# Weights of 512-column groups stored with two 128-column blocks interleaved, for a two-block transformer kernel on TensorE

## The reference

```python
mod_l = jax.nn.silu(c) @ w_ada + b_ada                    # 2048 x 12288, one row
p     = modulate(rms_norm(x, g), sh_a, sc_a) @ w_in       # 2048 x 3904
x     = x + gt_a * (merged_heads @ w_out)                 # 2048 x 2048
x     = x + gt_f * ((a * silu(g)) @ w_down)               # up 2048 x 11008, down 5504 x 2048
z     = rms_norm_2(x, norm_mix_g_2) @ w_in_2              # 2048 x 10248
x     = x + (sigmoid(g_a) * (att_a @ w_proj_a) + sigmoid(g_b) * (att_b @ w_proj_b)) @ w_out_2
x     = x + square(relu(hm @ w_up_2)) @ w_down_2          # 2048 x 8192 and back
```

## Time and profile before

| | |
|---|---|
| three timed runs | 2705.6, 2709.5, 2710.15 us |
| median | 2709.5 us |
| profiled execution, first to last instruction (its span) | 2701.8 us |
| busy: PE, weight loads, VectorE, ScalarE | 96%, 93%, 65%, 45% of the span |
| granted TensorE clock, mean | 0.984 |
| matmuls in the record | 21322 |
| HBM | 548.5 MB read, 204 GB/s over the span |

### The profile page before, as it was taken

One profiled execution on the slowest core, in us unless ns is written; L12 is line 12 of the kernel. 1 busy time (PEld: TensorE's weight loads), 2 busy tenths in 40 slices (PEclk: granted clock), 3 DMA queues, 4 the chain that ended last, 5 costly groups with the idle time before them and its releaser, 6 DMA issues.

```text
span 2701.8 us, 51009 instructions
## 1 busy us (share of the span) xinstructions
PE 2606.8 (96%) x21322; PEld 2522.5 (93%) x21322; DVE 1758.9 (65%) x2033; ACT 1222.5 (45%) x1487; POOL 112.5 (4%) x196
## 2 busy tenths in 40 slices
PE   6899988989999999999999999999999999999998
PEld 4699877889999999999999999999999999999997
DVE  5989776778888755665865655555665555555554
ACT  6753333345454544444544445444444444434433
POOL 0000323300000000000000110000000000000000
PEclk9899999989999999999999999999999999999999
DMA  9878766757777665565665555666566666666662
GB/s 353 283 227 271 254 210 206 240 174 242 250 242 250 208 198 173 168 220 175 197 189 155 180 159 160 194 194 193 192 183 195 193 195 194 189 194 195 194 210 95
DMA packets 289063, 553.55 MB, mean 205 GB/s; under 512 B 19386, under 2 KB 28712, under 8 KB 288232
## 3 DMA queue, kind: packets, MB, share of 16 engines
q1 hardware_dynamic: 288328, 548.53, 63.8%
q10 hardware_dynamic: 544, 2.29, 0.2%
HBM read 548.53 MB, written 2.10 MB: 204 GB/s over the span
## 4 chain that ended last, share of the span: by engine, by line
PE 84%; DVE 9%; ACT 3%; issue 2%; DMA 1%; POOL 1%; SPq 0%; ACTq 0%; DVEq 0%; POOLq 0%
PE half L1887 25%; PE half L1889 25%; PE half L1888 25%; DVE wlo L1100 4%; DMA raw<-in_w_ada 1%; ACT whi L618 1%; DVE acc L1129 1%; PE half L1921 1%; PE half L1923 1%; PE half L1922 1%; DVE acc L1132 1%; DVE tmp L1213 0%; PE half L2168 0%; PE half L2141 0%; PE half L2140 0%
## 5 line engine op out<-in xcount | busy, mean ns | idle before, releaser
L1100 DVE TENSOR_TENSOR wlo<-raw,whi 128x1024 fp32r<-128x1024 f32 (+1 forms) x909 | 1089.3, 1211 | 777.5 <-ACT whi L618 775.7
L618 ACT ACTIVATE whi<-raw 128x1024 fp32r<-128x1024 f32 (+1 forms) x909 | 940.5, 1048 | 1038.6 <-PE half L1889 922.6
L1887 PE MATMUL half<-hf,whi 128*128 128x256 f32 x2400 | 668.2, 278 | 6.4 <-DVE hf L1192 5.2
L1888 PE MATMUL half<-hf,whi 128*128 128x256 f32 x2400 | 666.2, 278 | 0.0
L1889 PE MATMUL half<-hf,wlo 128*128 128x256 f32 x2400 | 666.2, 278 | 0.0
L1887 PE MATMUL half<-hid,whi 128*128 128x256 f32 x1712 | 475.0, 277 | 1.2 <-DVE wlo L1100 1.2
L1888 PE MATMUL half<-hid,whi 128*128 128x256 f32 x1712 | 474.4, 277 | 0.0
L1889 PE MATMUL half<-hid,wlo 128*128 128x256 f32 x1712 | 474.4, 277 | 0.0
L1887 PEld LDWEIGHTS half<-hf,whi 128*128 128x128 f32 x2400 | 451.3, 188 | 8.5 <-issue 5.8
L1889 PEld LDWEIGHTS half<-hf,wlo 128*128 128x128 f32 x2400 | 453.0, 189 | 0.0
L1888 PEld LDWEIGHTS half<-hf,whi 128*128 128x128 f32 x2400 | 452.1, 188 | 0.0
(11 more groups left out here) (290 smaller groups left out, 3020.4 us busy)
## 6 DMA issues: line engine op xcount, KB each, us to landing
raw<-in_w_up SPq DMA_DIRECT2D x288, 512.0 KB, 4.3
raw<-in_w_in SPq DMA_DIRECT2D x216, 512.0 KB, 4.0
raw<-in_w_down SPq DMA_DIRECT2D x212, 512.0 KB, 4.5
raw<-in_w_ada SPq DMA_DIRECT2D x192, 512.0 KB, 5.2
raw<-in_w_out SPq DMA_DIRECT2D x64, 512.0 KB, 4.8
raw<-in_w_proj_a SPq DMA_DIRECT2D x16, 512.0 KB, 4.5
raw<-in_w_proj_b SPq DMA_DIRECT2D x16, 512.0 KB, 4.2
raw<-in_w_up SPq DMA_DIRECT2D x16, 384.0 KB, 3.4
```

The lines of the kernel that those rows point to most:

```text
L618: A(whi[:, s, 0:elems], raw[:, c, 0:elems], ACT.Copy).then_inc(s_hi_ready, 1)
L1100: V.tensor_tensor(wlo[:, s, 0:elems], raw[:, c, 0:elems], whi[:, s, 0:elems].bitcast(F32), ALU.subtract).then_inc(s_drained, 1)
L1887: mm(o, hi, x[:, 0:T], start=(k == 0 and b % 2 == 0), stop=False, skip_group_check=True)
L1888: mm(o, hi, x[:, T:2 * T], start=False, stop=False, skip_group_check=True)
```

## The change

Chunks whose length is a multiple of 512 words are split into a woven order, unless the caller asks for the straight one: of each 256 columns (two blocks of 128), word 2n is column n of the first block and word 2n + 1 column n of the second. ScalarE writes `whi` in that order, VectorE reads `whi` and writes `wlo` in it; `raw` is read contiguously as before. `product` with 512-column groups takes every second word of 256 as its stationary block. The groups that are read in another way keep the straight order (`split_straight`). The number and order of all instructions, loads and semaphores stays as it is.

```diff
+        def woven(t, s, elems):
+            return t[:, s, 0:elems].rearrange("p (a n q) -> p a q n", n=P, q=2)
+
+        def straight(t, c, elems):
+            return t[:, c, 0:elems].rearrange("p (a q n) -> p a q n", n=P, q=2)
+
+        def woven_block(w, at):
+            pair = w[:, at - at % (2 * P):at - at % (2 * P) + 2 * P].rearrange("p (n q) -> p q n", q=2)
+            return pair[:, at // P % 2, :]
...
@@ ScalarE
-            def split(elems):
+            def split(elems, weave=True):
...
-                A(whi[:, s, 0:elems], raw[:, c, 0:elems], ACT.Copy).then_inc(s_hi_ready, 1)
+                if weave and elems % GW == 0:
+                    A(woven(whi, s, elems), straight(raw, c, elems), ACT.Copy).then_inc(s_hi_ready, 1)
+                else:
+                    A(whi[:, s, 0:elems], raw[:, c, 0:elems], ACT.Copy).then_inc(s_hi_ready, 1)
...
+            def split_straight(elems):
+                split(elems, False)
...
-            ahead(KVB, turn)
+            ahead(KVB, turn, split=split_straight)
...
@@ VectorE
-                V.tensor_tensor(wlo[:, s, 0:elems], raw[:, c, 0:elems], whi[:, s, 0:elems].bitcast(F32),
-                                ALU.subtract).then_inc(s_drained, 1)
+                if weave and elems % GW == 0:
+                    V.tensor_tensor(woven(wlo, s, elems), straight(raw, c, elems), woven(whi, s, elems).bitcast(F32),
+                                    ALU.subtract).then_inc(s_drained, 1)
+                else:
+                    V.tensor_tensor(wlo[:, s, 0:elems], raw[:, c, 0:elems], whi[:, s, 0:elems].bitcast(F32),
+                                    ALU.subtract).then_inc(s_drained, 1)
...
@@ TensorE, product
+                part = woven_block if width == GW else (lambda w, at: w[:, at:at + P])
...
-                            ins_ = block(folded(half(nth))[:, b, :], b, hi[:, at:at + P], lo[:, at:at + P], src(k), k, nk)
+                            ins_ = block(folded(half(nth))[:, b, :], b, part(hi, at), part(lo, at), src(k), k, nk)
```

More of the change, by code:

```diff
@@ L748, in _ @@
             for g in range(8):
-                ahead(STD, turn if g > 0 else None, side={c: replies[GC * g + c] for c in range(GC) if GC * g + c in replies})
+                ahead(STD, turn if g > 0 else None, split=split_straight, side={c: replies[GC * g + c] for c in range(GC) if GC * g + c in replies})
             def norm_both():
@@ L866, in _ @@
             ahead(QBG, lambda: conv_in(0), split=split_pair)
-            ahead(KVB, turn, side={0: q_root()})
+            ahead(KVB, turn, side={0: q_root()}, split=split_straight)
             ahead(STD, lambda: turn(2), None, CONV_SUMS[1])
             ahead(QBG, lambda: conv_in(1), split=split_pair)
-            ahead(KVB, turn)
+            ahead(KVB, turn, split=split_straight)
             ahead(STD, lambda: turn(2), None, CONV_SUMS[2], side={6: att1})
@@ L1013, in _ @@
                 ahead(STD, turn, side={2: roots()} if s == 0 else side[1])
-                ahead(STD, turn, side=side[2])
+                ahead(STD, turn, side=side[2], split=split_straight)
                 if s == 1:
@@ L1272, in _ @@
             for g in range(8):
-                ahead(STD, mod_rows if g > 0 else None, (lambda: mod_cols(4 * g - 4)) if g > 0 else None,
+                ahead(STD, mod_rows if g > 0 else None, (lambda: mod_cols(4 * g - 4)) if g > 0 else None, split=split_straight,
                       side={c: replies[GC * g + c] for c in range(GC) if GC * g + c in replies})
@@ L1520, in _ @@
             ahead(QBG, lambda: conv_in(0), split=split_pair)
-            ahead(KVB, lambda: queries(0), side={0: q_root()})
+            ahead(KVB, lambda: queries(0), side={0: q_root()}, split=split_straight)
             ahead(STD, lambda: first_values(0), mod, CONV_SUMS[1], side={5: rotate(0)}, third=(1, lambda: keys(0)))
             ahead(QBG, lambda: conv_in(1), split=split_pair)
-            ahead(KVB, lambda: queries(1))
+            ahead(KVB, lambda: queries(1), split=split_straight)
             ahead(STD, lambda: first_values(1), mod, CONV_SUMS[2], side={5: rotate(1), 6: att1}, third=(1, lambda: keys(1)))
@@ L1527, in _ @@
             ahead(QBG, lambda: conv_in(3), split=split_pair, side={1: att1})
-            ahead(KVB, lambda: queries(2))
+            ahead(KVB, lambda: queries(2), split=split_straight)
             def both(*parts):
@@ L1536, in _ @@
             ahead(QBG, lambda: conv_in(5), split=split_pair, side={1: att1})
-            ahead(KVB, lambda: queries(3))
+            ahead(KVB, lambda: queries(3), split=split_straight)
             ahead(WIDE, lambda: first_values(3), None, WIDE_SUMS,
@@ L1730, in _ @@
                       (lambda: norm_x(0 if s == 0 else 3)) if s < 2 else None,
-                      side={} if s == 0 else {1: before, 4: before})
+                      side={} if s == 0 else {1: before, 4: before}, split=split_straight)
                 if s == 1:
```

## The result

The changed kernel takes 2792.94 us (median of 4 runs, 2791.66 to 2793.19), the kernel before 2707.55 us (its three timed runs and, as the fourth, the profiled execution, entered with its span of 2701.8 us). The ratio is 1.0314, 95% interval 1.03 to 1.0329: 85 us slower, and 88 us from span to span. The forecast was 53 us slower, 2760 us, in a range of 2675 to 2850.

A forecast was written before the change was run, and what follows sets the result against it. The prediction took PE's interval between matmul starts as the bound; 53 us for the slower load, zero for the 118 ns stretches and the passes, added to 2709.5 us, gave about 2760 us, range 2675 to 2850.

The forecast's parts named there:

- What bounds the kernel: PE, busy 96% of the span: time is the number of matmuls times the interval between their starts.
- Loads within 2 ns of the bound: On TensorE a load takes 111 ns against the 113.3 ns moving read; one slower by over 2 ns delays each matmul.
- The stationary read: Product's stationary block spread over 1024 bytes, as the moving operand: load grows 6 ns, its interval from 111 to 117.5 ns.
- The interval: Matmuls at the 113 ns pace go to 117.5 ns: 4.2 ns on each of 12500, 53 us.
- The number 12500: Touched product matmuls put at the 113 ns pace, some two thirds of 18768.
- The 118 ns stretches at zero cost: The other 6250 touched matmuls, at 117.6 to 118 ns: the load ends no later than now, cost 0.
- Nothing hidden: Before 600 us part hides behind waits for VectorE, but PE is busy 243.81 of 259 us: nothing taken off.
- ScalarE's and VectorE's passes: Split passes of 1058 and 1223 ns, now at a two-word step: taken as zero, bounds zero to 0.8 us a pass.
- All at the 113 ns pace: Rival on TensorE: woven, both reads keep clear of each other, giving back 27 us: 2682 us, chance 0.30.
- The worse collision: Rival on TensorE: the 118 ns pace's extra 4.4 ns doubles for all, 136 us: 2845 us, chance 0.06.
- Nothing happens: Rival on the stationary load: paced by the array, two hits on a line suffice: 2709 us, chance 0.17.
- A line for every word: Rival on the stationary load: every word costs a line, interval 211 ns, 1800 us more: 4500 us, chance 0.06.

The follow-up runs named there:

- e2: Kernel before, contiguous split, only the product's stationary read changed to every second word of 256: 2792.41 us, 1.0323 of the kernel before.
- e7: Changed kernel, second and third of each three matmuls load and use 64 of 128 stationary columns: 2764.08 us.
- e9: Changed kernel, second and third of each three matmuls stream 128 instead of 256 moving columns: 3408.16 us, mean granted clock 0.771.
- e1: Changed kernel with woven writing kept and the product reading 128 contiguous words as stationary block: 2711.61 us, 1.0028 of the kernel before.
- e5: Kernel before, stationary block is one word repeated 128 times (step 0): 2691.69 us, 0.9953 of the kernel before.
- e8: Kernel before, second and third of each three matmuls load and use 64 of 128 stationary columns, contiguous: 2689.03 us.
- e10: Kernel before, second and third of each three matmuls stream 128 instead of 256 moving columns: 3324.5 us, mean granted clock 0.778.

## Why the prediction was right, point by point

*What bounds the kernel.* Right. The starts of PE's matmuls set the time: e2 moves the whole time by touching nothing but PE's read, and its count of matmuls from 2003 to 2633 us falls with it, from 5561 to 5249.

*Loads within 2 ns of the bound.* Borne out in the outcome: 6 ns on a load of 188 became 6.8 ns on the interval of the 113 ns stretches. It isn't the whole reason: e7 loses 5 of these 6.8 ns though two of its three loads are far from the bound.

*The stationary read.* The longer load and its size were right: 194 ns were forecast and 194 are shown. The reason given, that 1024 bytes can't be fetched sooner than the moving read fetches them, holds for the 16-byte stretches in them rather than for the bytes: the steps of 4 and 8 tell the two apart. It rests on 113.3 ns being the pace of the moving read; the 8-column row that was read so only says that it isn't the load's.

*The interval.* Mis-sized, and by a term that the sum put at nothing. It was 117.5 ns, the load alone, and e9 has 117.6 with the moving read cut in two of three; with the whole moving read beside the load it is 120.1. The sum left out that the two reads delay one another: 2.5 ns on 12500 matmuls, 31 us. The 4.3 and 2.5 ns are the forecast's own way of dividing the 6.8. They aren't two measured causes, for in e7 the delay alone is worth more than the 2.5, by estimate 3.6 ns (118.3 less the 114.7 of the loads' own length). The number 12500 held: counted in the trace of the kernel before by runs of 24 product matmuls, 520 of 725 go at 113 to 114 ns, 12480 matmuls, and 186 at 117 to 119.

*The 118 ns stretches at zero cost.* Wrong, small: they went to 119.8, 2 ns on 6250 matmuls, 13 us.

*Nothing hidden.* Wrong, and on the other side. The three terms make 12500 x 6.8 + 6250 x 2 = 98 us, and the span grew by 88 (spans are the fair measure here: of the 7.7 us that the forecast took to lie around an execution only 1.8 do, as the changed kernel's profiled execution shows with 2791.66 us for a span of 2789.9; the rest is the spread between executions). In the first 600 us, where PE waits for others, the changed kernel (second row) starts as many matmuls as the kernel before, but for 5:

```profile
0.00:600.00 600.00, 521.39 (x3644) 0.94 0.75 250
```

```profile
0.00:600.00 600.00, 527.39 (x3639) 0.95 0.75 250
```

PE is busy 6 us longer there and waits 6 us less, so the waits hid at least that much; the rest of the 10 us can lie there too, or in the granted clock, which was a little higher. The forecast saw this hiding and took nothing off. That it came within 32 to 35 us of the result is in part luck, since the terms left out, 31 and 13 us, and the 10 us that were hidden pull in opposite ways.

*ScalarE's and VectorE's passes.* VectorE's at zero was right. ScalarE's, put at zero, grew by 102 ns, which lies between my bounds, and its cover held (e1).

*The rivals.* All at the 113 ns pace: refuted by the 119.8 ns; its idea, that the 118 ns pace is a collision, has the runs behind it in part (e5, e8), but the woven read didn't keep clear of the moving one. The worse collision, which had a chance of 0.06, was nearest to the truth in kind, and the measured time lies between the forecast's 2760 and its 2845 us: e7 shows a collision that needs no long load. Its doubling of the 4.4 ns wasn't seen, and the longer load is there as well. Nothing happens: refuted. There the Trainium skill, SBUF — State Buffer, section "Door 1: The DMA port swizzle", has full bandwidth for two hits on each line of 16 bytes; e2's loads, with two hits a line, take 194 ns and its matmuls 120.0, and ScalarE's pass takes 1160 ns in the changed kernel instead of 1058, so for these two engines the measurement decides against it. For VectorE, 1225 against 1223 ns, it holds. A line for every word: refuted for a step of two, and true for steps of 4 and 8, where 4901 us stand against my 4500.

## What to carry to other kernels

Before laying out an operand at a step, count the 16-byte stretches that it touches, and compare them, at some 1.8 to 1.9 ns each at the full clock, with the time that its elements take anyway. In a kernel that reloads 128 fp32 columns for each 256 moving ones, both sides stand within a few ns of that limit, so here a contiguous stationary block was worth 3% against a step of two, and a step of four cost 80%. Look for a row of the same engine that touches as much memory as the new pattern will: here the moving operand gave the growth of the load to the nanosecond. What it didn't give is how two such reads share, and only a run with both reads whole shows that.

## What the runs showed of the hardware

- A stationary load of 128 fp32 words costs, at the full clock, the larger of 0.83 ns a column and 1.82 to 1.88 ns for each 16-byte stretch touched: shown for 188 ns at steps 0 and 1, 194 at 2, 260 at 3, 325 at 4, 332 at 8, with 117.6, 174.3, 232.8 and 240.7 ns from load to load at steps 2, 3, 4 and 8.
- The moving read of 256 fp32 words in the reduced format takes 113.3 ns contiguous and 219 to 232 ns at a step of two.
- The two reads disturb each other. The kernel before has a long stretch at 117.6 ns that goes to 113.1 with one stationary word (e5) and is gone with 64 stationary columns (e8); stepped loads of 64 columns hold the interval at 118.3 (e7). What keeps one stretch at one pace and the next at the other is open.
- ScalarE's pass of 1024 fp32 words takes 1141 (e1) to 1160 ns (the changed kernel) instead of 1058 when it writes at a step of two words, 8 to 10% more; VectorE's takes 1225 instead of 1223.
- With half the moving columns in two of three matmuls the granted clock stood at 0.50, 1.2 GHz, for long stretches (e9, e10), though PE was busy 222 of 222 us there; with 256 columns in all three it stood at 1.00 in the same window. There a woven and a straight load cost the same, 213 ns.
